# Layer 0's projection: who evicts its products, and where the modulation parts are summed

## What is computed

```python
mod = jnp.split((jax.nn.silu(c) @ ada_w[l] + ada_b[l])[:, None, :], 6, axis=-1)
mod_c = jnp.split(jax.nn.silu(c_ctx) @ ada_w[l] + ada_b[l], 6, axis=-1)
h = modulate(x, norm1_g[l], mod[0], mod[1])
hc = modulate(xc, norm1_g[l], mod_c[0], mod_c[1])
...
p = split_proj(h @ w_in)
pc = split_proj(hc @ w_in)
```

## Time and profile before

| | us |
|---|---|
| runs shown (three): median | 4508.95 |
| lowest and highest | 4507.74 and 4509.69 |
| the profiled execution | 4507.21 |
| its span on the core | 4505.4 |
| PE busy in the span | 2254.4 |
| DVE busy in the span | 2614.6 |
| POOL busy in the span | 2604.7 |
| ACT busy in the span | 462.0 |

### The profile page before, as it was taken

How to read it: one execution, slowest core, us unless ns; L and a number is a source line. 1 busy time by engine, 2 the same in 40 slices (tenths; PEclk the granted TensorE clock), 3 DMA queues, 4 the chain that set the end, 5 groups by cost and what they waited for, 6 DMA issues and landing times. The chain is left out here.

```text
span 4505.4 us, 35616 instructions
## 1 busy us (share of the span) xinstructions
PE 2254.4 (50%) x11749; PEld 1085.6 (24%) x11749; DVE 2614.6 (58%) x5877; ACT 462.0 (10%) x944; POOL 2604.7 (58%) x2779
## 2 busy tenths in 40 slices
PE   7997887562052051151155787698454025035035
PEld 2434654220010010010013644475221001001001
DVE  2115568597945946846846700556867972963930
ACT  1004540110000000000000000352110000000000
POOL 1103305777777777777767563220777767767765
PEclk9997899886576576576577898789786568568556
DMA  6941026999999999999999998203999999999998
GB/s 221 277 163 38 22 111 222 400 409 409 410 407 409 409 399 409 409 399 409 409 402 407 400 399 337 103 2 114 370 409 409 410 409 409 410 405 400 410 409 332
DMA packets 454373, 1496.76 MB, mean 332 GB/s; under 512 B 60931, under 2 KB 94295, under 8 KB 448047
## 3 DMA queue, kind: packets, MB, share of 16 engines
q0 software_dynamic: 368640, 1342.34, 75.3%
q1 hardware_dynamic: 48104, 82.26, 5.3%
q10 hardware_dynamic: 37446, 69.88, 4.6%
HBM read 1476.58 MB, written 17.73 MB: 332 GB/s over the span
## 5 line engine op out<-in xcount | busy, mean ns | idle before, releaser
L2416 DVE CUSTOM_DVE_ANT_0 experts_V<-experts_V,experts_acc 128x1024 f32<-128x1024 f32 x512 | 621.1, 1220 | 488.2 <-DMA experts_V<-in_peer_u_dram,experts_expert 470.1
L1807 POOL DMA_INDIRECT experts_lent<-in_peer_u_dram,experts_expert x576 | 560.3, 973 | 581.6 <-DVE experts_expert L1556 385.8
L1814 POOL DMA_INDIRECT experts_V<-in_peer_v_dram,experts_turned x576 | 545.4, 947 | 262.1 <-issue 153.0
L2211 PE MATMUL experts_pair<-small,experts_w 128*128 128x128 f32 x12 | 5.6, 463 | 1278.6 <-DVE experts_w L2372 1177.9
L2416 DVE CUSTOM_DVE_ANT_0 experts_lent<-experts_lent,experts_acc 128x1024 f32<-128x1024 f32 x512 | 620.1, 1220 | 42.2 <-DMA experts_lent<-in_peer_u_dram,experts_expert 23.3
L2228 PE MATMUL experts_acc<-experts_lent,experts_U 128*32 128x512 f32 x1968 | 456.4, 816 | 330.2 <-DMA experts_lent<-in_peer_v_dram,experts_turned 174.8
L1807 POOL DMA_INDIRECT experts_V<-in_peer_u_dram,experts_expert x512 | 485.3, 948 | 172.3 <-issue 98.4
L1814 POOL DMA_INDIRECT experts_lent<-in_peer_v_dram,experts_turned x492 | 468.5, 952 | 185.5 <-issue 125.5
L2228 PE MATMUL experts_acc<-experts_V,experts_U 128*32 128x512 f32 x2304 | 386.6, 802 | 282.6 <-DMA experts_V<-in_peer_v_dram,experts_turned 282.6
L2211 PEld LDWEIGHTS experts_pair<-small,experts_w 128*128 128x128 f32 x12 | 2.1, 178 | 1282.0 <-DVE experts_w L2372 1179.7
L429 PE MATMUL proj_acc<-W,HT 128*128 128x512 f32 (+3 forms) x752 | 295.4, 547 | 5.5 <-DMA W<-in_w_in_dram 3.2
(11 more groups left out here) (299 smaller groups left out, 3794.3 us busy)
## 6 DMA issues: line engine op xcount, KB each, us to landing
proj_ada<-in_ada_w_dram ACTq DMA_DIRECT2D x40, 1024.0 KB, 5.7
W<-in_w_in_dram SPq DMA_DIRECT2D x9, 2048.0 KB, 14.8
experts_QT<-in_w_in_dram ACTq DMA_DIRECT2D x12, 960.0 KB, 18.4
experts_lent<-in_peer_u_dram,experts_expert POOLq DMA_INDIRECT x576
experts_V<-in_peer_v_dram,experts_turned POOLq DMA_INDIRECT x576, 12.9
PR<-in_ada_w_dram SPq DMA_DIRECT2D x8, 1024.0 KB, 17.3
experts_U<-in_w_out_dram SPq DMA_DIRECT2D x4, 2048.0 KB, 9.0
experts_V<-in_peer_wq_dram SPq DMA_DIRECT2D x4, 2048.0 KB, 18.0
```

Source lines behind the costliest of these rows:

```text
L1807: pool.indirect_dma_start(into, None, u_rows, bass.IndirectOffsetOnAxis(ap=s.expert[:, j % 2, slot:slot + 1], axis=0)).then_inc(done, 16)
L1814: pool.indirect_dma_start(into, None, v_rows, bass.IndirectOffsetOnAxis(ap=s.turned[:, q % 2, at:at + 1], axis=0)).then_inc(done, 16)
L2211: nc.tensor.transpose(tr[:, P:2 * P], s.w[:], m.ident).then_inc(wtr, 1)
L2416: nc.vector.tensor_tensor_reduce(out=rows, in0=rows, in1=s.H[:, tiles[0]] if q == 0 and k < FROM_BANK else h_bank(), scale=1.0, scalar=0.0 ...
```

## The change

In layer 0's projection only:

- ScalarE's stream now evicts all 42 products (line 547, `ACT.Copy`). After the evictions named by `LOAD_AT` it asks for the next `ada_w` blocks: within part p, block k is asked for behind product 7p + LOAD_AT[k]. The two-buffer ring stays; load n now waits for `scaled`, VectorE's work on step n - 2. Its first instructions are the eight bias loads and the first two `ada_w` loads, then the evictions. Stores and bias loads stay at their blocks (k = 4 and k = 7).
- VectorE evicts nothing in layer 0. For each block it multiplies the 128 x 2048 block by one column of `silu`, for each of the two vectors, and adds it to a sum in SBUF (`sums`, in `scratch[:, 0:4]`): two instructions per step, `tensor_scalar` for k = 0 (line 568) and `scalar_tensor_tensor` for k = 1 to 7 (line 571). It adds biases after the second step of the next part (line 498).
- PE has no ada steps. Once per part, after products 10, 17, 24, 31 and 38, it sums `sums` over the partitions: 2 x 4 matmuls (line 518) against a column of ones. It waits first for all 16 VectorE instructions of the part. VectorE waits for that sum before it starts the next part, because `sums` exists once.

Layer 1's projection keeps its form.

```diff
+    ADA_ITEMS, PARTS = 7, ((0, 1), (0, 2), (1, 0), (1, 1), (1, 2))
+    LOAD_AT, SUM_AT = [2, 3, 5, 6, 6, 7, 8, 8], 10
...
+            def loads_behind(i):
+                return [KD * p + k for p in range(len(PARTS)) for k in range(KD) if ADA_ITEMS * p + LOAD_AT[k] == i and KD * p + k >= AR]
...
             @block.tensor
             def _(pe):
                 for i in range(EARLY, len(work)):
                     product(pe, i)
-                    for n in ada_steps(i):
-                        pe.wait_ge(adas[n % AR], 16 * (n // AR + 1))
-                        if n and n % KD == 0:
-                            pe.wait_ge(added, 4 * (n // KD))
-                        ada_strips(nc, m, mod, ada[:, n % AR], n % KD).then_inc(used, 1)
+                    p = part_summed(i)
+                    if p is None:
+                        continue
+                    pe.wait_ge(scaled, 2 * KD * (p + 1))
...
+                    for x in range(2):
+                        for strip in range(4):
+                            mm = nc.tensor.matmul(mod[32 * strip:32 * strip + 2], one[:, x], sums[:, x, 512 * strip:512 * strip + 512],
+                                                  start=x == 0, stop=x == 1)
+                    mm.then_inc(used, 1)
 
             @block.scalar
...
                     if n >= AR:
-                        act.wait_ge(used, n - AR + 1)
-                    p, k = n // KD, n % KD
+                        act.wait_ge(scaled, 2 * (n - AR + 1))
...
+                for p in range(2):
+                    ada_bias(act, m, rows[:, p], *PARTS[p], biases[p])
+                for n in range(AR):
+                    load_ada(n)
+                for i, (c, t) in enumerate(work):
+                    c0, wd, _ = chunks[c]
+                    act.wait_ge(prods, i + 1)
+                    nc.scalar.activation(PR[:, t, c0:c0 + wd], acc[:, i % BANKS, 0:wd], ACT.Copy).then_inc(ev, 1)
+                    for n in loads_behind(i):
+                        load_ada(n)
...
             @block.vector
             def _(dve):
...
+                for n in range(ADA_N):
+                    dve.wait_ge(adas[n % AR], 16 * (n // AR + 1))
+                    if n and n % KD == 0:
+                        dve.wait_ge(used, n // KD)
+                    for x in range(2):
+                        factor = m.silu[:, x, n % KD:n % KD + 1]
+                        if n % KD == 0:
+                            ins = nc.vector.tensor_scalar(sums[:, x], ada[:, n % AR], factor, None, ALU.mult)
+                        else:
+                            dve.wait_ge(scaled, 2 * n - 1 + x)
+                            ins = nc.vector.scalar_tensor_tensor(out=sums[:, x], in0=ada[:, n % AR], scalar=factor, in1=sums[:, x],
+                                                                 op0=ALU.mult, op1=ALU.add)
+                        ins.then_inc(scaled, 1)
```

More of the change, by code:

```diff
@@ L406, in project @@
             adas = [st.sem(f"ada{i}") for i in range(AR)]
-            used, added, stored = (st.sem(x) for x in ("used", "added", "stored"))
+            used, added, stored, scaled, ones = (st.sem(x) for x in ("used", "added", "stored", "scaled", "ones"))
             biases = [st.sem(f"biases{b}") for b in range(2)]
+            one = st.sb("one", [P, 2, 2])
+            sums = scratch[:, 0:4].rearrange("p (s a) n -> p s (a n)", s=2)
             table = scratch[:, 5, 0:14 * GRID_W].rearrange("p (r c) -> p r c", c=GRID_W)
@@ L485, in project, with add_bias, part_summed @@
             ADA_N = len(PARTS) * KD if first else 0
[L487 to L492, removed]
+            def loads_behind(i):
+                return [KD * p + k for p in range(len(PARTS)) for k in range(KD) if ADA_ITEMS * p + LOAD_AT[k] == i and KD * p + k >= AR]
+            def add_bias(dve, p):
+                dve.wait_ge(biases[p % 2], 64 * (p // 2 + 1))
+                dve.wait_ge(used, p + 1)
+                for strip in range(4):
+                    row = rows[32 * strip:32 * strip + 2, p % 2]
+                    nc.vector.tensor_tensor(row, row, mod[32 * strip:32 * strip + 2], ALU.add).then_inc(added, 1)
+            def part_summed(i):
+                p, at = divmod(i - SUM_AT, ADA_ITEMS)
+                return p if first and at == 0 and 0 <= p < len(PARTS) else None
             @block.tensor
@@ L497, in _ @@
                     product(pe, i)
[L498 to L502 removed]
+                    p = part_summed(i)
+                    if p is None:
+                        continue
+                    pe.wait_ge(scaled, 2 * KD * (p + 1))
+                    if p:
+                        pe.wait_ge(added, 4 * p)
+                    else:
+                        pe.wait_ge(ones, 3)
+                    for x in range(2):
+                        for strip in range(4):
+                            mm = nc.tensor.matmul(mod[32 * strip:32 * strip + 2], one[:, x], sums[:, x, 512 * strip:512 * strip + 512],
+                                                  start=x == 0, stop=x == 1)
+                    mm.then_inc(used, 1)
             @block.scalar
@@ L507, in _, with load_ada @@
                     return
-                for p in range(2):
-                    ada_bias(act, m, rows[:, p], *PARTS[p], biases[p])
-                for n in range(ADA_N):
+                def load_ada(n):
+                    p, k = n // KD, n % KD
                     if n >= AR:
-                        act.wait_ge(used, n - AR + 1)
-                    p, k = n // KD, n % KD
+                        act.wait_ge(scaled, 2 * (n - AR + 1))
                     if p and k == KD // 2:
@@ L527, in _ @@
             def _(dve):
+                if first:
+                    nc.vector.memset(one[:], 0.0).then_inc(ones, 1)
+                    dve.wait_ge(ones, 1)
+                    for x in range(2):
+                        nc.vector.memset(one[:, x, x:x + 1], 1.0).then_inc(ones, 1)
+                for n in range(ADA_N):
+                    dve.wait_ge(adas[n % AR], 16 * (n // AR + 1))
+                    if n and n % KD == 0:
+                        dve.wait_ge(used, n // KD)
+                    for x in range(2):
+                        factor = m.silu[:, x, n % KD:n % KD + 1]
+                        if n % KD == 0:
+                            ins = nc.vector.tensor_scalar(sums[:, x], ada[:, n % AR], factor, None, ALU.mult)
+                        else:
+                            dve.wait_ge(scaled, 2 * n - 1 + x)
+                            ins = nc.vector.scalar_tensor_tensor(out=sums[:, x], in0=ada[:, n % AR], scalar=factor, in1=sums[:, x],
+                                                                 op0=ALU.mult, op1=ALU.add)
+                        ins.then_inc(scaled, 1)
+                    if n % KD == 1 and n > KD:
+                        add_bias(dve, n // KD - 1)
+                if first:
+                    add_bias(dve, len(PARTS) - 1)
+                    return
                 for i, (c, t) in enumerate(work):
@@ L531, in _ @@
                     nc.vector.tensor_copy(PR[:, t, c0:c0 + wd], acc[:, i % BANKS, 0:wd]).then_inc(ev, 1)
[L532 to L540, removed]
 SMALL = P + 256 + GRID_W + 16
```

1 line of the change is left out of this document (removed).

## The result

The changed kernel takes 4539.84 us (median of four runs, 4536.46 to 4542.02) against 4508.34 us of the kernel before in the same comparison: a ratio of 1.0067, 95% interval 1.0055 to 1.0080. The forecast was 4531 us in a range of 4504 to 4550. The profiled execution took 4542.02 us, its span is 4540.2 us.

The account below looks back on a forecast made before the run. TensorE sets the pace now; with the change the two-buffer ring's chains hold it. Start 2.6, products 229.1, sums 10.3, waits 53.6, clock 11.5 us put the next stage at 394.2 against 372.3: +21.9 us, 4531 us (4504 to 4550).

Parts of the forecast that it names:

- The chain: Layer 0's projection: in each part blocks 3, 5 and 7, three links from block 3's request, end last; the sum waits.
- The removal: TensorE in layer 0's projection loses 37 ada steps of 1.18 us (43.7 us), a 2.0 us stall, 10.3 us at the end.
- The start: Product 3 waits for ScalarE's first eviction behind bias and ada_w loads: 2.6 us later, TensorE standing 4.1 us there.
- VectorE's step: Two instructions over 2048 elements at 2.36 us each, 4.7 us a step; 2.4 us for a part's first step.
- Landings and links: A link is landing plus 4.7 plus 0.1 us; narrow part landing 6.6, link 11.4 us; quiet 9.7, at most 12.2.
- The waits: TensorE before the sums: 19.2, 21.0, 5.5, 5.5 and 2.4 us, together 53.6 us (37.2 to 67.2).
- The clock: TensorE at 1.2 GHz after idling: 2.3 us at the start and behind four sums waiting over 4 us, 11.5 us.
- POOL: Eight table subtractions may block VectorE's two-input instructions: none in the forecast, 9.6 us in the upper end.
- Nothing later changes: Stages behind layer 0's projection keep their times, so the stage's +21.9 us is the whole program's change.
- The quiet rival: Ada_w landings all near 4.9 us, fewer clock drops: next stage 1 us later, about 4510 us; chance 0.18.
- the fast-VectorE rival: VectorE at 1.2 us an instruction, link 9.1 us: next stage 10 us earlier, 4499 us; chance 0.11.
- The rival in which contention adds up: Links of 12.2, waits of 67.2, clock 11.5 us, eight POOL collisions: +45 us, 4554 us; chance 0.11.

Follow-up runs that it names:

- The last experiment: Changed kernel with three buffers, early requests, sums placed by time, early first evictions, and one window table fewer ahead of the chunk 3 request: 4464.07 us, ratio 0.9897.
- the two-buffer schedule: Changed kernel, still two buffers, each block requested when its buffer comes free, sums behind products 10, 20, 27, 33 and 40: 4481.28 us, ratio 0.9940.

## Why the forecast was right, and where its sizes were off

- **The chain.** The forecast said that the chain of blocks 3, 5 and 7 ends last in each part. In part 0 that is wrong: blocks 2, 4 and 6 and then step 7 set the sum. That the wait still came out at 20.7 against 19.2 us is partly luck. Without POOL's subtractions both chains end within 0.2 us of each other (block 7 landed at 139.20, step 6 ended at 139.36), so they are about equally long, and landings shorter than assumed made up for part of the collisions. What carries the forecast, that each request stands behind a step and the links add up, holds in both chains, and earlier requests or a third buffer take the wide parts' waits away.
- **The removal.** 37 steps at 1.18 us and a 14.6 us end: the sum without waits gave a next stage at 329.1. The last experiment, with 1.6 us of waiting left and the first evictions early, has it at 326.9. The term holds to a few us. The end took 399.03 - 395.24 = 3.8 us behind the last product, forecast 4.3.
- **The start.** Product 3 started at 84.72 with 4.10 us of idling ahead of it, as foretold; it followed the turned tiles, which were 0.8 us earlier than in the earlier trace rows.
- **VectorE's step.** 2.346 us against 2.36 from the earlier trace rows; the first step of a part 2.48 for two against 2.4.
- **Landings and links.** I took 6.6 us for the narrow part. The loads issued between 105 and 170 landed in 5.9 us (median), between 170 and 286 in 5.4, later in 4.9, where the earlier trace rows has 7.4, 6.3 and 4.8: quieter than I took them. The chains came out longer all the same, for two reasons that the sum left at nought: collisions with POOL (1.3 and 1.8 us in part 0), and the store or the bias loads that ScalarE issues inside the chain. In part 1, for one, block 15's request at 188.67 stands behind a bias issue of 1.17 us at 187.47.
- **The waits.** 20.7 and 22.1 us before sums 0 and 1 (forecast 19.2 and 21.0). Before sums 2 and 3 6.8 and 9.8 (forecast 5.5 each): the load of `W`, asked for at 244.56 and 296.38 with table reads right behind it, falls on the last link each time; which of the two held the blocks back isn't separated. Blocks 23 and 31 were asked for at 245.56 and 302.83 and worked on from 253.57 and 313.37, 8.0 and 10.5 us later. A mean over landings missed that the traffic meets the chain at its end. Bias issues of 1.2 us stand ahead of both requests as well, and step 31 met a subtraction (4.16 us). Before sum 4: 0.9 against 2.4. Together 60.3 against 53.6.
- **The clock.** Behind waits of 6.8 us and more a sum took 3.5 to 3.6 us instead of 1.90, and the granted clock of that stretch is 0.50, the 1.2 GHz level. Four sums cost 6.7 us so, the products of the stretches behind them and at the start some 4 us more (41.66 us where three wide and five narrow products make 39.9; 48.88 where 48.33 is usual). Forecast 11.5 in all, found near 10.5. The forecast charged waits of over 4 us; other runs show that the length of a wait alone doesn't decide. A sum behind 2.26 us ran 3.33 us in the two-buffer schedule and one behind 2.49 us ran 3.20 without subtractions, while one behind 3.40 us ran 1.90 us at clock 1.00 with the requests moved.
- **POOL.** I gave the collisions no place in the forecast and 9.6 us at the upper end. In the stage the run without subtractions is 3.9 to 6.4 us shorter, with the reservation above. This is the term that was mis-sized most in proportion. The rule of the Trainium skill (SBUF — State Buffer, the section on its two separate sides) is borne out in both directions: line 571 took up to 4.17 us, and POOL's subtractions up to 3.87 us against 2.08 before.
- **Nothing later changes.** This step fell in part. The stage gives 26.7 and 26.1 us of 34.8 and 32.4 us in the spans. Some 2 us lie in `gla`, with the clock at its lower level for longer; the rest isn't settled: both traces of the kernel before are short behind the projection, both of the changed one long, while variants with the same changed instructions cover 4128 to 4142 us.

In sum the forecast of +21.9 us stood 4.8 us under the stage's +26.7. The waits, POOL's collisions among them, were 6.7 us longer than forecast; the start, the clock and the end took about 2 us less. The quiet rival was wrong since its links had no POOL and no W load in them; the fast-VectorE rival fell with the 2.346 us. The rival in which contention adds up (+45 us) went too far: landings stayed under its 7.4 us in the middle, the waits came to 60.3 and not 67.2 us, and the collisions reached the stage's end with less than 9.6.

## What to carry to other kernels

When a step moves from the engine that sets the pace to an idle one, add up the chain that now feeds the idle engine (request, landing, work, next request), not its busy time: VectorE's multiplications took 185 us (177 in the forecast) beside a loop of 242 us without waits, and TensorE still waited 60 us. With a ring of two buffers each request stands behind a step, so ask for a block the moment its buffer is free, and place the points where the fast engine collects results by time, not by a count of work items of unequal length. When a loss goes, look what is late next: here it was a weight load queued behind a table.

## What the runs showed of the hardware that I had not expected

- A VectorE instruction with two SBUF inputs and a POOL instruction with SBUF inputs don't share time: 2.35 us became up to 4.17, and POOL's 2.08 up to 3.87. Where VectorE ran its instructions without a gap between them (the run without loads), one POOL subtraction took 7.64 us.
- A TensorE clock at its lower level delays the engine that feeds TensorE, too: behind a slow sum (3.6 us) VectorE's next part began 3.79 us after its last step, and behind a sum of 1.9 us, with the requests moved, 2.1 us after it.
- Leaving 38 of the 40 loads out gained less (26.6 us under the kernel before) than asking for all of them in time did (29.8 and, with the third buffer and SP's order, 48.1). The latter runs moved the sums too; without the loads one wait of 17.9 us stayed before a sum that stood too early.
